# Twenty places for expert weights in place of eighteen, and new homes for the buffers ahead of the expert loop

## The chip, the cores and the metric

The kernel runs on one core of a Trainium2 chip. Its engines work side by side, each on its own stream of instructions, and wait for one another on semaphores: PE (TensorE, matrix products), DVE (VectorE), ACT (ScalarE), POOL (GpSimd) and SP (SyncE, which here only issues loads and stores). Data lies in DRAM, in SBUF (128 partitions, from which the engines read) and in PSUM, where PE leaves its results. Sixteen DMA engines move data between DRAM and SBUF. The metric is the time of one execution in microseconds (us) on the device; lower is better. A MB of weights is 1,048,576 bytes here; megabytes in the profile are millions of bytes.

## The reference

One streaming step of an encoder layer for 288 tokens (256 of a prompt, 32 of a sample) with 1024 channels, all in 32-bit floats. A conditioning vector for each of the two groups gives shifts, scales and gates. Ahead of the experts stand a normalization, an input projection, a pooling mixer, a convolution module, sigmoid gates and an output projection. What takes most of the time is the last part, a mixture of 32 experts, of which each token is given to four:

```python
h2 = RMSNorm(x) * (1 + scale2(c)) + shift2(c)
logits = (h2 @ router_w + router_b); top_vals, top_idx = top_k(logits, 4); top_w = softmax(top_vals)
for e in range(32):
    gt = minimum(t @ exp_w_gate[e] + exp_b_gate[e], 7.0)
    up = clip(t @ exp_w_up[e] + exp_b_up[e], -7.0, 7.0)
    act = gt * sigmoid(1.702 * gt) * (up + 1.0)
    out = out + combine[:, e:e + 1] * (act @ exp_w_down[e] + exp_b_down[e])
y = RMSNorm(x + gate2(c) * out)
```

Each expert has three matrices of 1024 x 1024 floats, 4 MB each, so the weights of all 32 are 384 MB, and each byte is used for the few tokens that chose the expert.

## The kernel before

**The front** is everything up to the router. Its weights come in 46 pieces of up to 1 MB (`FRONT`), in the order in which PE uses them, into a ring of twelve places of 1 MB. SP issues the loads; the load of a piece waits until PE has used what lay in its place, which PE counts in the semaphore `piece_used`. The other buffers of the front lie in one large tile, `arena`, as views at fixed offsets; several views share the same bytes at different times. The tokens `x` and the normalized tokens `h2` are tiles of their own.

**The experts.** Tokens are gathered into groups of at most 64 for one expert; such a group is an item. There are at least 32 items, and one more for each expert that has over 64 tokens. One item (`item`) is three products on PE (gate, up, down), each over four pieces of 1 MB; beside them stand the scatter of the item before, the gather of the next item, and transposes. DVE and ACT do the clamps, the sigmoid and the sums in between. The matrices of an expert come in six pairs of pieces: gate 0 and 1, up 2 and 3, down 4 and 5. Pairs are numbered through all experts (`q`), and pair q goes to place q modulo `PAIRS`: the six pairs of places of the ring, and three pairs of places in the arena, EARLY, LATE and LAST. With nine pairs and six to an expert the assignment repeats after three experts (`TURN`), so the loops of PE and SP are written out for three experts, run ten times, and two experts follow behind. An expert's items are an inner loop whose bounds are read from a table.

**The order of the loads on SP** is one queue. Behind the last pieces of the front come the pairs of expert 0 in the order 5, 0, 1, 2, 3, 4, each when PE has used what lay in its places of the ring; pair 4 in two halves. Between pairs 1 and 2 comes the first pair of expert 1, into EARLY (it waits for the convolution's activations and two more). After pair 4 come the second pair of expert 1 into LATE, when the logits of all tokens are there (`logit_mm`), and the third into LAST, when the last tokens are normalized (`h2_ready`). Then SP waits for the table of the items (`base_ready`) and from there on refills places (`refill`): pair q is loaded when PE has used pair q - 9. The first three of these go in halves (`refill_halves`, `HALVED`).

**Around the change on ACT and DVE.** ACT spreads rows of the modulation from DRAM to all partitions (`spread`: `g1b`, `sh2b`, `a2b`). DVE adds the output projection to `x` (`add_output`), normalizes (`norm2`) first the sample rows (tile 2) and later tile 0, and picks experts (`choose`). ACT takes squares and roots in between. Copies of the sample rows to `xs` stand on ACT right ahead of the loop.

Of the kernel before, what the change touches and what calls it, by code (L numbers as in the profile page):

```python
# [24 lines left out]
P = 128  # L25
# [30 lines left out]
ARENA = 17660  # L56
EARLY_PAIR, LATE_PAIR, LAST_PAIR = ARENA - 4096, 7168, 3072
# [3 lines left out]
PAIRS = 9  # L61
TURN = 3
SPLIT, HALVED, LAST_HALVES = 4, 3, (1, 2, 3, 5)
# [22 lines left out]
def build(nc, x_prompt, x_sample, state_pool, state_conv, c_prompt, c_sample, norm1_g, norm2_g, final_g,  # L86
# [3 lines left out]
    with ExitStack() as ctx:  # L90
# [8 lines left out]
        x = sb("x", [P, TT, D])  # L99
        h2 = sb("h2", [P, TT, D])  # L100
# [10 lines left out]
        c_cols = sb("c_cols", [P, 2 * KD])  # L111
# [5 lines left out]
        csig = sb("csig", [P, 16])  # L117
# [29 lines left out]
        hT = view(0, KD, TOK)  # L147
        gates = view(2304, 2 * KD, TOK)
        hS = view(2304, KD, TOK)
        shT = view(8064, KD, 32)  # L150
        group_of = view(8320, TOK)
        pick = view(8608, 2, 2)
        merged = view(6912, KD, TOK)
        sig_g = view(6912, CT, TOK)
        up_ext = view(9216, CT, PEXT)
        pooled = view(10488, CT, TOK)
        wsum = view(11640, 2, PEXT)
        rows = view(12288, 3, HALF)
        tmp = view(13824, CT, CW)
        act_c = view(9216, CT, TOK)  # L160
        slot_i = view(13824, SLOTS).bitcast(I32)
        part_i = view(13824 + SLOTS, SLOTS).bitcast(I32)
        n2rows = view(15120, HALF)[0:64, :]
        bada = view(15632, HALF)[0:4, :]
        ada_sel = view(16144, 4, 32)[0:4, :, :]
        ada_bias = [view(16912, HALF), rows[:, 0, :]]
        stage = view(16528, P)[0:N_COLS, :]
        c_stage = view(16656, P)[0:2 * KD, :]
        dwc = view(16784, CT, 32)
        h2flat = h2[:, :, :].rearrange("p a b -> p (a b)")  # L170
        uc_ext = h2flat[:, 0:CT * CEXT].rearrange("p (a b) -> p a b", b=CEXT)
        yc = h2flat[:, CT * CEXT:CT * CEXT + CT * CW].rearrange("p (a b) -> p a b", b=CW)


        g1b = view(0, 2, D)
        a2b = view(2304, 2, D)
        sh2b = view(4352, 2, D)
        g2h = biases[:, 1, :].rearrange("p (a n) -> p a n", a=2)
        x2T = view(9216, KD, 2 * P)
        x2T_s = cT  # L180
        rw_g = [view(2048, KD, E), rw]
        junk = view(6400, HALF)
        junk2 = view(11776, HALF)
        ysb = view(11264, 2, HALF)
        xs = view(12672, D // 4)
        part_sum = view(13504, 4)
        xg = view(0, HALF)
        xgT = view(512, HALF)
        ohwT = view(12288, TT * P)
        gmin = view(1024, HALF)  # L190
        gsig = view(1536, HALF)
        acts = view(2048, HALF)
        actT = view(2560, HALF)
        bias_down = ysb[:, 0, :]
        same_row = view(12928, P)
        y_s = h2[:, 2, 0:D // 4]
        oh = view(13312, TT, SLOTS)
        turned = view(13056, 2 * TT, 32)
        count_b = view(2560, P)[0:E, :]
# [9 lines left out]
        ybuf = h2  # L209
        ln_mean, ln_var = view(6912, CW), view(6912 + CW, CW)  # L210

        def slots(q, k):

            if q < RING:
                return ring[:, q:q + k, :].rearrange("p s n -> p (s n)")
            at = (EARLY_PAIR, LATE_PAIR, LAST_PAIR)[(q - RING) // 2] + SLOT * (q % 2)
            return arena[:, at:at + SLOT * k]
# [5 lines left out]
        far_ld = [sem(f"far_ld{i}") for i in range(3)]  # L223
        pair_ld = slot_ld[0:RING:2] + far_ld

        def half_at(p):

            return 2 * p + 1 if 2 * p < RING else 2 * p - RING // 2 + 1
# [71 lines left out]
        h2_zero = sem("h2_zero")  # L300
# [153 lines left out]
        def _(sp):  # L454
# [78 lines left out]
            for i, t in enumerate((0, 2, 1)):  # L533
# [4 lines left out]
                elif t == 0:  # L538
                    sp.dma_start(y_prompt[0, 0:P, :], ybuf[:, 0, :]).then_inc(stored, 16)
                else:  # L540
                    for hh in range(2):
                        sp.wait_ge(y_ready, i + 1 + hh)
                        cs = slice(HALF * hh, HALF * (hh + 1))
                        sp.dma_start(y_prompt[0, P:2 * P, cs], ybuf[:, 1, cs]).then_inc(stored, 16)
# [4 lines left out]
        def _(pool):  # L549
# [82 lines left out]
            pool.wait_ge(pm_mm, KD)  # L632
# [4 lines left out]
        def _(act):  # L637
# [12 lines left out]
            for t in range(2):  # L650
                act.wait_ge(x_ld[t], 16)
                a.activation(view(2304 + D * t, D), x[:, t, :], ACT.Square, accum_out=stat[:, t:t + 1]).then_inc(ssq, 1)
# [6 lines left out]
            a.activation(h2[:, 1, :], x[:, 1, :], ACT.Copy, scale=stat[:, 5:6]).then_inc(xn_ready, 1)  # L659
# [95 lines left out]
            def spread(buf, b, at, done):  # L755
                for gg, r in ((0, P), (1, NS_TOK)):
                    act.dma_start(buf[0:r, gg, :], mod_rows[b][gg:gg + 1, D * at:D * (at + 1)].broadcast_to([r, D])) \
# [30 lines left out]
            a.activation(h2[0:NS_TOK, 2, :], x[0:NS_TOK, 2, :], ACT.Square, accum_out=stat[0:NS_TOK, 2:3]).then_inc(ssq2, 1)  # L788
            act.wait_ge(ssq2, 1)
            root(2, 1)  # L790
            for hh in range(2):
                cs = slice(HALF * hh, HALF * (hh + 1))
                act.wait_ge(x2_ready, 2 + hh)
                a.activation(h2[:, 0, cs], x[:, 0, cs], ACT.Square, accum_out=stat[:, 12 + hh:13 + hh]).then_inc(ssq2, 1)
# [4 lines left out]
            root(0, 2)  # L799
            act.wait_ge(x2_ready, 4)  # L800
# [63 lines left out]
        def _(dve):  # L864
# [16 lines left out]
            squares = view(2304 + 2 * D, D)[0:NS_TOK, :]  # L881
# [13 lines left out]
            for t in (0, 2):  # L895
                r = ROWS[t]
                v.tensor_scalar(h2[0:r, t, :], x[0:r, t, :], stat[0:r, 4 + t:5 + t], None, ALU.mult).then_inc(xn_ready, 1)
# [120 lines left out]
            v.memset(h2[:, 2, :], 0.0).then_inc(h2_zero, 1)  # L1018
# [43 lines left out]
            v.memset(item_col[:, :, :], 0.0)  # L1062
            dve.wait_ge(rows_out[1], 64)
            step(v.memset(oh, 0.0))
            step(v.memset(rt[:, 6, 2, :], 1.0))

            dve.wait_ge(h2_zero, 1)
            wo_reads = [0]

            def add_output(r, t, cuts, after=0):  # L1070
# [3 lines left out]
                parts = [view(12288 + cs.start, cs.stop - cs.start)[0:r, :] for cs, _ in cuts]  # L1074
                for part, (cs, src) in zip(parts, cuts):
                    v.tensor_tensor(part, src, g1b[0:r, t // 2, cs], ALU.mult).then_inc(wo_ev, 1)
# [6 lines left out]
            def norm2(t):  # L1083

                r, gg = ROWS[t], t // 2
                step(v.scalar_tensor_tensor(out=h2[0:r, t, :], in0=x[0:r, t, :], scalar=stat[0:r, 4 + t:5 + t],
                                            in1=a2b[0:r, gg, :], op0=ALU.mult, op1=ALU.mult))
                v.tensor_tensor(h2[0:r, t, :], h2[0:r, t, :], sh2b[0:r, gg, :], ALU.add).then_inc(h2_ready, 1)
# [39 lines left out]
            choose(2, 1)  # L1128
            dve.wait_ge(ssq2, 3)
# [747 lines left out]
```

## Time and profile before

| what | us |
|---|---|
| three runs | 1151.28, 1152.16, 1153.07 |
| median of the runs | 1152.16 |
| the profiled execution, first to last instruction (span) | 1150.3 |
| median less span, taken for what lies around it | 1.9 |
| PE busy | 1122.8 (98%) |
| DVE, ACT, POOL busy | 497.9 (43%), 181.4 (16%), 29.8 (3%) |
| moved by DMA | 456.15 MB, mean 397 GB/s |

The profile is of one execution. Its page shows the span in 40 equal slices of 28.8 us; a chain of waits, followed back from the last instruction, says at each moment what the end was waiting for; groups and timelines give single instructions by line, engine and operation, with the tiles that they write and read (out<-in) and, in brackets, the idle time ahead of them and what ended it. ACTq and SPq are the instructions by which ACT and SP issue DMA; their duration is that of the issue, not of the transfer. In a row with xN the duration runs from the start of the first of the N to the end of the last. Matmuls of PE are pipelined; each 32-bit product counts as two matmuls and two weight loads (PEld).

### The profile page before, as it was taken

The numbers are of one execution on the slowest core, as the hardware profiler recorded it, in microseconds if no ns is written. First come the engines' busy times: TensorE is split into PE (matmuls) and PEld (weight loads), VectorE is DVE, ScalarE is ACT, GpSimd is POOL, SyncE is SP. The second block draws the span as 40 slices with busy tenths as digits, with TensorE's granted clock in tenths as the row PEclk, the third lists the DMA queues.
The fourth block names the chain that finished last, engine by engine and source line by source line (L and its number), as shares of the span: only waits on it lengthen the run. The fifth ranks groups of instructions, "written<-read, shape, count | busy, mean of one in ns | idle before, by whom it ended". The sixth has DMA issues, their size and how long they took to land.

```text
span 1150.3 us, 16135 instructions
## 1 busy us (share of the span) xinstructions
PE 1122.8 (98%) x5962; PEld 457.5 (40%) x5963; DVE 497.9 (43%) x1134; ACT 181.4 (16%) x343; POOL 29.8 (3%) x78
## 2 busy tenths in 40 slices
PE   8999999999999999999999999999999999999996
PEld 6676675633333333333333333333333333333332
DVE  3498425653344433444333433343334433333334
ACT  4101301311111111111111111111111111111112
POOL 4002300000000000000000000000000000000000
PEclk9999999999999999999999999999999999999999
DMA  9988688699999999999999999999999999999995
GB/s 342 374 288 297 245 305 303 229 419 417 427 428 428 428 428 428 428 428 428 428 428 428 428 428 428 428 428 428 428 428 428 428 428 428 428 428 429 426 422 228
DMA packets 59022, 456.15 MB, mean 397 GB/s; under 512 B 7237, under 2 KB 26497, under 8 KB 31349
## 3 DMA queue, kind: packets, MB, share of 16 engines
q1 hardware_dynamic: 54880, 452.35, 94.9%
q10 hardware_dynamic: 4117, 3.47, 1.2%
q8 instruction: 16, 0.26, 0.1%
q14 instruction: 9, 0.07, 0.0%
HBM read 454.40 MB, written 1.40 MB: 396 GB/s over the span
## 4 chain that ended last, share of the span: by engine, by line
PE 77%; DMA 21%; DVE 1%; issue 0%; SPq 0%; ACT 0%; DVEq 0%
PE bank L1731 46%; DMA arena<-in_exp_w_up 10%; DMA arena<-in_exp_w_gate 10%; PE bank L1509 6%; PE bank L1456 4%; PE bank L1758 4%; PE bank L1675 4%; PE bank L1596 2%; PE bank L1813 1%; PE bank L1579 1%; PE bank L1683 1%; PE bank L1430 1%; PE bank L1749 1%; PE bank L1687 1%; PE bank L1378 1%; PE bank L1689 0%
## 5 line engine op out<-in xcount | busy, mean ns | idle before, releaser
L1731 PE MATMUL bank<-ring,arena 128*64 128x512 f32 x2112 | 469.9, 595 | 10.2 <-DMA ring<-in_exp_w_gate 9.7
L1731 PEld LDWEIGHTS bank<-ring,arena 128*64 128x64 f32 x2112 | 146.3, 137 | 310.0 <-issue 283.7
L1731 PE MATMUL bank<-arena 128*64 128x512 f32 x1056 | 235.9, 595 | 4.2 <-DMA arena<-in_exp_w_gate 4.0
L1731 PEld LDWEIGHTS bank<-arena 128*64 128x64 f32 x1056 | 73.6, 137 | 153.8 <-issue 138.5
L821 ACT ACTIVATE arena<-arena 32x256 f32<-32x256 f32 x136 | 56.0, 412 | 421.1 <-DVE arena L1200 419.9
L1291 DVE TENSOR_SCALAR arena<-bank 128x512 f32<-128x512 f32 x33 | 22.8, 691 | 166.6 <-PE bank L1731 166.6
L1284 DVE TENSOR_SCALAR arena<-bank 128x512 f32<-128x512 f32 x33 | 22.8, 691 | 166.5 <-PE bank L1731 166.5
L1306 DVE TENSOR_TENSOR arena<-bank,biases 128x512 f32<-128x512 f32 x66 | 42.5, 686 | 109.9 <-PE bank L1731 109.9
L1269 DVE TENSOR_TENSOR x<-x,bank 128x512 f32<-128x512 f32 x132 | 84.5, 681 | 12.6 <-PE bank L1758 12.6
L834 ACT ACTIVATE arena<-arena 128x512 f32<-128x512 f32 x33 | 20.8, 629 | 353.8 <-DVE arena L1284 353.8
L1758 PE MATMUL bank<-arena 64*128 64x512 f32 x264 | 65.6, 615 | 0.0
L1509 PE MATMUL bank<-arena,ring 128*128 128x288 f32 x256 | 64.4, 409 | 0.0
L1675 PE MATMUL bank<-h,arena 128*64 128x512 f32 x268 | 63.3, 592 | 0.0
L969 DVE SCALAR_TENSOR_TENSOR h<-h,arena 128x318 f32<-128x318 f32 x120 | 55.5, 541 | 0.0
L1509 PEld LDWEIGHTS bank<-arena,ring 128*128 128x128 f32 x256 | 48.1, 190 | 17.1 <-issue 4.2
L1456 PE MATMUL bank<-arena,ring 128*128 128x288 f32 x192 | 47.7, 408 | 0.5 <-DVE arena L922 0.5
L834 ACT ACT_TABLE_LOAD x33 | 42.3, 1283 | 0.6
L1456 PEld LDWEIGHTS bank<-arena,ring 128*128 128x128 f32 x192 | 36.2, 190 | 12.0 <-issue 1.7
L1687 PE MATMUL bank<-biases,mine 32*64 32x288 f32 x264 | 40.0, 414 | 0.0
L1758 PEld LDWEIGHTS bank<-arena 64*128 64x128 f32 x264 | 22.7, 186 | 42.3 <-issue 42.3
L1205 DVE COPY arena<-arena 32x256 f32<-32x256 f32 x136 | 38.4, 282 | 2.5
L1683 PE MATMUL bank<-biases,mine 32*64 32x512 f32 x136 | 37.4, 613 | 0.0
(312 smaller groups left out, 739.8 us busy)
## 6 DMA issues: line engine op xcount, KB each, us to landing
ring<-in_exp_w_gate SPq DMA_DIRECT2D x42, 2048.0 KB, 27.8
ring<-in_exp_w_up SPq DMA_DIRECT2D x41, 2048.0 KB, 28.2
ring<-in_exp_w_down SPq DMA_DIRECT2D x40, 2048.0 KB, 29.1
arena<-in_exp_w_gate SPq DMA_DIRECT2D x21, 2048.0 KB, 25.7
arena<-in_exp_w_up SPq DMA_DIRECT2D x20, 2048.0 KB, 27.3
arena<-in_exp_w_down SPq DMA_DIRECT2D x20, 2048.0 KB, 30.0
ring<-in_w_ada SPq DMA_DIRECT2D x24, 1024.0 KB, 10.7
ring<-in_gate_w SPq DMA_DIRECT2D x8, 1024.0 KB, 8.6
```

Source lines behind the costliest of these rows:

```text
L821: ins = a.activation(*square_moves(1, s, u), ACT.Copy)
L834: a.activation(gsig, gmin, ACT.Sigmoid, scale=ALPHA).then_inc(gsig_ready, 1)
L969: ins = v.scalar_tensor_tensor(out=yc[:, c, :], in0=uc_ext[:, c, k:k + CW], scalar=tap, in1=yc[:, c, :], op0=ALU.mult, op1=ALU.add)
L1269: ins = v.tensor_tensor(x[:, t, cs], x[:, t, cs], scatter_bank(t, hh), ALU.add)
L1306: v.tensor_tensor(ysb[:, gg, :], bank[5][:, :], g2h[:, gg, :], ALU.mult).then_inc(y_ev, 1)
L1456: ins = mm(bank[n % 4][:, 0:TOK], w[:, k, P * (n % 2):P * (n % 2 + 1)], (hS if n < UNSHIFTED else hT)[:, k, :], start=(k == 0), stop=(n >= ...
L1509: ins = mm(bank[n % 4][:, 0:TOK], w[:, k, P * (n % 2):P * (n % 2 + 1)], hT[:, k, :], start=(k == 0), stop=(k == KD - 1))
L1675: ins = mm(bank[0][64 * hh:64 * hh + 64, :], oh[:, t, :], half_rows(h2[:, t, :], hh), start=start, stop=stop, skip_group_check=True)
L1683: mm(bank[3][out, :], mine[B_GATE, :], bias_rows[B_GATE, cs], start=True, stop=False, skip_group_check=True)
L1687: found = mm(bank[6 + i][out, 0:TOK], mine[LOOKUP, :], routedT[:, i, :], start=True, stop=True, skip_group_check=True)
L1731: ins = mm(out[64 * hh:64 * hh + 64, :], lhs(k), w[:, D * (k % 2) + HALF * hh:D * (k % 2) + HALF * (hh + 1)], start=(done is y_mm and k == ...
L1758: ins = mm(scatter_bank(t, hh), ohwT[64 * hh:64 * hh + 64, P * t:P * (t + 1)], ysb[64 * hh:64 * hh + 64, 0, :], start=True, stop=True, ski ...
```

## The change

Nothing that is computed changes. The arena grows from 17660 to 23840 columns and takes in `x` and `h2`, which were tiles of their own; its views are laid out anew, so that four pairs of places lie in it: EARLY as before, SAMPLE where tile 2 of `x` and the sample's modulation rows lie, MERGED where the merged branches lie, and NORM, whose first half holds the convolution's activations and whose second half holds modulation rows of the prompt. That is ten pairs of places. The assignment of pairs now repeats after five experts, and the loops of PE and SP are written out for five, run six times, with two experts behind. The constants and the views (the other views are moved likewise):

```diff
-ARENA = 17660
-EARLY_PAIR, LATE_PAIR, LAST_PAIR = ARENA - 4096, 7168, 3072
+MERGED_PAIR = WEIGHTED_AT + 288
+NORM_PAIR = MERGED_PAIR + 4096
+EARLY_PAIR = NORM_PAIR + 4096
+SAMPLE_PAIR = 2 * D
+ARENA = EARLY_PAIR + 4096
-PAIRS = 9
-TURN = 3
-SPLIT, HALVED, LAST_HALVES = 4, 3, (1, 2, 3, 5)
+PAIRS = 10
+TURN = 5
+SPLIT, HALVED, LAST_HALVES = 4, 2, (1, 2, 3, 5)
+NORM_SPLIT = 9
...
-        x = sb("x", [P, TT, D])
-        h2 = sb("h2", [P, TT, D])
+        x = view(TOKENS_AT, TT, D)
+        h2 = [view(NORMED_AT + D * t, D) for t in range(2)] + [biases[0:NS_TOK, 0, :]]
+        sh2b = [view(NORM_PAIR + SLOT + D, D), view(SAMPLE_PAIR + D, D)]
+        a2b = [view(NORM_PAIR + SLOT, D), view(SAMPLE_PAIR + 2 * D, D)]
+        g1b = [h2[1], view(SAMPLE_PAIR + 3 * D, D)]
```

The loads on SP (`order` is the order 5, 0, 1, 2, 3, 4 of the pairs of expert 0):

```diff
+            def load_half(e, q, half):
+                i, p = q % PER_EXPERT, q % PAIRS
+                w = (wg_v, wu_v, wd_v)[i // 2]
+                sp.dma_start(slots(2 * p + half, 1), w[e][:, i % 2, SLOT * half:SLOT * (half + 1)]).then_inc(pair_ld[p], 16)
...
+                if i == order[4]:
+                    sp.wait_ge(cm_mm, KD)
+                    load_half(1, NORM_SPLIT, 0)
+                    sp.wait_ge(h2_ready, 1)
+                    sp.wait_ge(xs_ready, 1)
+                    load(1, PER_EXPERT + 1)
                 if i == SPLIT:
                     for half in range(2):
-                        sp.wait_ge(piece_used, front_use(i) - 1 + half)
+                        if half:
+                            sp.wait_ge(wo_mm, 6)
+                        else:
+                            sp.wait_ge(piece_used, front_use(i) - 1)
...
-            sp.wait_ge(logit_mm, TT)
-            load(1, PER_EXPERT + 1)
+            sp.wait_ge(ssq2, 6)
+            load(1, PER_EXPERT + 2)
             sp.wait_ge(h2_ready, TT + 1)
-            load(1, PER_EXPERT + 2)
+            load_half(1, NORM_SPLIT, 1)
             sp.wait_ge(base_ready, 1)
```

On the other engines: ACT's copies of the sample rows move up, behind the root of tile 0, and write where the router's weights lay; DVE clears its one-hot tile `oh` behind the choice for the sample and no longer ahead of the output projection, and drops a memset of `h2`; POOL's memset of `bias_down` waits for the merged branches in place of the pooling product; ACT waits for `rows_out` one spread earlier.

```diff
             act.wait_ge(merged_ready, KD)
+            act.wait_ge(rows_out[1], 64)
             spread(sh2b, 0, 1, spread_ld[1])
-            act.wait_ge(rows_out[1], 64)
...
             root(0, 2)
+            act.wait_ge(logit_mm, 1)
+            for q in range(4):
+                ins = a.activation(quadrant(xs, q), quarter(x[0:NS_TOK, 2, :], q), ACT.Copy)
+            ins.then_inc(xs_ready, 1)
             act.wait_ge(x2_ready, 4)
...
             move_squares()
-            act.wait_ge(h2_ready, TT + 1)
-            for q in range(4):
-                ins = a.activation(quadrant(xs, q), quarter(x[0:NS_TOK, 2, :], q), ACT.Copy)
-            ins.then_inc(xs_ready, 1)
...
             choose(2, 1)
+            step(v.memset(oh, 0.0))
```

How this stands on SP, from the last pieces of the front to the table of the items. Before (a place in `ring` or `arena`, the matrix, its shape, and the semaphores that end the wait):

```order
L469 DMA ring<-in_exp_w_down 128x4096 [waits piece_used]
L469 DMA ring<-in_exp_w_gate 128x4096 [waits piece_used] x2
L469 DMA arena<-in_exp_w_gate 128x4096 [waits rows_out2,cst_mm,act_c_ready]
L469 DMA ring<-in_exp_w_up 128x4096 [waits piece_used] x2
L486 DMA ring<-in_exp_w_down 128x2048 [waits piece_used] x2
L469 DMA arena<-in_exp_w_gate 128x4096 [waits logit_mm]
L469 DMA arena<-in_exp_w_up 128x4096 [waits h2_ready]
L510 TENSOR_LOAD base_i [waits base_ready]
```

And on SP now, the same stretch:

```order
L481 DMA ring<-in_exp_w_down 128x4096 [waits piece_used]
L481 DMA ring<-in_exp_w_gate 128x4096 [waits piece_used] x2
L481 DMA arena<-in_exp_w_gate 128x4096 [waits rows_out2,cst_mm,act_c_ready]
L481 DMA ring<-in_exp_w_up 128x4096 [waits piece_used]
L487 DMA arena<-in_exp_w_up 128x2048 [waits cm_mm]
L481 DMA arena<-in_exp_w_gate 128x4096 [waits xs_ready,h2_ready]
L481 DMA ring<-in_exp_w_up 128x4096 [waits piece_used]
L514 DMA ring<-in_exp_w_down 128x2048 [waits piece_used]
L514 DMA ring<-in_exp_w_down 128x2048 [waits wo_mm]
L481 DMA arena<-in_exp_w_up 128x4096 [waits ssq2]
L487 DMA arena<-in_exp_w_up 128x2048 [waits h2_ready]
L538 TENSOR_LOAD base_i [waits base_ready]
```

A half for NORM and a whole pair for SAMPLE have moved between the two up pairs of expert 0, and behind the down halves there are a pair for MERGED and the other half for NORM, where there were two pairs.

On ACT, from the squares of the sample rows to the squares of tile 1, before:

```order
L788 ACTIVATE h,stat<-x 32x1024 [waits x2_ready]
L784 ACTIVATE stat<-stat 32x1 [waits ssq2]
L794 ACTIVATE h,stat<-x 128x512 [waits x2_ready]
L797 ACTIVATE arena<-bank 128x4x128 [waits x2_turned]
L794 ACTIVATE h,stat<-x 128x512 [waits x2_ready]
L784 ACTIVATE stat<-stat 128x1 [waits mean2]
L801 ACTIVATE arena,stat<-x 128x512 [waits x2_ready]
```

And on ACT now (`x` and `h2` are part of `arena`, the normalized sample rows of `biases`, `xs` of `rw`):

```order
L816 ACTIVATE biases,stat<-arena 32x1024 [waits x2_ready]
L812 ACTIVATE stat<-stat 32x1 [waits ssq2]
L822 ACTIVATE arena,stat<-arena 128x512 [waits x2_ready]
L825 ACTIVATE arena<-bank 128x4x128 [waits x2_turned]
L822 ACTIVATE arena,stat<-arena 128x512 [waits x2_ready]
L812 ACTIVATE stat<-stat 128x1 [waits mean2]
L830 ACTIVATE rw<-arena 32x256 [waits logit_mm]
L830 ACTIVATE rw<-arena 32x256 x3
L833 ACTIVATE arena,stat<-arena 128x512 [waits x2_ready]
```

Four copies have moved in between the root of tile 0 and the squares of tile 1.

## Rows read from the trace of the kernel before

**Rows 1.** The page: span, GB/s in 40 slices, a group of the loop.

```profile
span 1150.3 us, 16135 instructions
...
GB/s 342 374 288 297 245 305 303 229 419 417 427 428 428 428 428 428 428 428 428 428 428 428 428 428 428 428 428 428 428 428 428 428 428 428 428 428 429 426 422 228
...
L1291 DVE TENSOR_SCALAR arena<-bank 128x512 f32<-128x512 f32 x33 | 22.8, 691 | 166.6 <-PE bank L1731 166.6
```

**Rows 2.** Stretches: PE, PEld, DVE, ACT, POOL busy (count); PE clock, DMA share, GB/s.

```profile
197.30:209.00 11.70, 11.70 (x51) 6.16 (x50) 5.50 (x14) 1.61 (x4) 0.00 (x0) 1.00 0.02 7
...
219.00:220.50 1.50, 1.50 (x13) 1.33 (x12) 1.36 (x4) 0.87 (x3) 0.00 (x0) 1.00 0.03 11
220.50:231.00 10.50, 10.15 (x70) 5.71 (x72) 8.80 (x39) 6.74 (x14) 0.00 (x0) 1.00 0.99 370
231.00:246.50 15.50, 15.50 (x78) 5.11 (x76) 9.65 (x32) 0.63 (x1) 0.00 (x0) 1.00 1.00 419
246.50:270.00 23.50, 23.50 (x130) 8.12 (x128) 9.76 (x22) 3.97 (x7) 0.00 (x0) 1.00 1.00 407
...
300.00:1100.00 800.00, 786.27 (x4180) 266.81 (x4178) 310.60 (x668) 115.19 (x203) 0.00 (x0) 1.00 1.01 428
```

**Rows 3.** Chain that ended last, 300 to 1130 us: start, us, what.

```profile
542.80 38.62 DMA arena<-in_exp_w_gate
...
1070.74 39.47 DMA arena<-in_exp_w_gate
1110.35 7.09 PE bank L1731 x32
```

**Rows 4.** Stretches of one item each, from the loop's start (columns as above).

```profile
228.88:255.82 26.94, 26.94 (x144) 9.39 (x146) 14.98 (x47) 5.94 (x10) 0.00 (x0) 1.00 1.00 416
...
309.69:336.62 26.93, 26.93 (x146) 9.26 (x144) 10.71 (x23) 3.97 (x7) 0.00 (x0) 1.00 1.01 428
```

**Rows 5.** SP's issues, 120 to 320 us: start, us, engine, line, op, tiles.

```profile
181.96 27.10 SPq L469 DMA_DIRECT2D ring<-in_exp_w_up  x2
214.37 5.74 SPq L486 DMA_DIRECT2D ring<-in_exp_w_down  x2
221.31 0.33 SPq L469 DMA_DIRECT2D arena<-in_exp_w_gate  x1
224.70 0.33 SPq L469 DMA_DIRECT2D arena<-in_exp_w_up  x1
230.86 2.05 SPq L513 DMA_DIRECT2D ring<-in_exp_w_up  x2
234.29 8.12 SPq L513 DMA_DIRECT2D ring<-in_exp_w_down  x4
246.53 6.59 SPq L469 DMA_DIRECT2D ring<-in_exp_w_gate  x2
```

**Rows 6.** Timeline of ACT and DVE: start, us, operation, idle ahead and its end.

```profile
182.40 2.33 ACTq L757 DMA_DIRECT2D arena<-mod_rows  x4
...
197.21 1.27 DVE L1086 SCALAR_TENSOR_TENSOR h<-x,stat,arena 32x1024 f32<-32x1024 f32 x1 [3.32 <-DMA arena<-mod_rows]
...
202.51 0.29 ACT L784 ACTIVATE stat<-stat 128x1 f32<-128x1 f32 x1 [0.59 <-DVE stat L1130]
...
208.31 0.69 DVE L1132 COPY arena<-bank 128x512 f32<-128x512 f32 x1 [5.83 <-PE bank L1606]
...
213.01 0.63 ACT L801 ACTIVATE arena<-x 128x512 f32<-128x512 f32 x1 [10.21 <-DVE x L1080]
...
227.88 1.69 ACT L828 ACTIVATE arena<-x 32x256 f32<-32x256 f32 x4
```

**Rows 7.** Instruction queues (PE's is q8) in 228.9-309.7, 309.7-1085, 1085-1150.3 us.

```profile
q8 instruction: 4, 0.07, 0.3%
...
q14 instruction: 1, 0.01, 0.0%
...
q8 instruction: 3, 0.05, 0.3%
```

More of the change, by code:

```diff
@@ L144, in view @@
             return a
[L147 to L177, printed above, removed]
+        def front(start, *shape):
+            return view(FRONT_AT + start, *shape)
+        x = view(TOKENS_AT, TT, D)
+        xn = view(OLD_ROWS_AT, TT, D)
+        uc_ext = view(OLD_ROWS_AT, CT, CEXT)
+        yc = view(OLD_ROWS_AT + CT * CEXT, CT, CW)
+        hT = view(OLD_ROWS_AT + 2688, KD, TOK)
+        gates = front(2304, 2 * KD, TOK)
@@ new lines, in build @@
+        hS = front(2304, KD, TOK)
+        shT = front(8064, KD, 32)
+        group_of = front(8320, TOK)
+        pick = front(8608, 2, 2)
+        merged = front(6912, KD, TOK)
+        sig_g = front(6912, CT, TOK)
+        up_ext = front(9216, CT, PEXT)
+        pooled = front(10488, CT, TOK)
+        wsum = front(11640, 2, PEXT)
+        rows = front(12288, 3, HALF)
+        tmp = front(13824, CT, CW)
+        act_c = front(9216, CT, TOK)
+        slot_i = front(13824, SLOTS).bitcast(I32)
+        part_i = front(13824 + SLOTS, SLOTS).bitcast(I32)
@@ new lines, in build @@
+        n2rows = front(15120, HALF)[0:64, :]
+        bada = front(15632, HALF)[0:4, :]
+        ada_sel = front(16144, 4, 32)[0:4, :, :]
+        ada_bias = [front(16912, HALF), rows[:, 0, :]]
+        stage = front(16528, P)[0:N_COLS, :]
+        c_stage = front(16656, P)[0:2 * KD, :]
+        dwc = front(16784, CT, 32)
+        c_cols = front(17424, 2 * KD)
+        csig = front(17440, 2 * KD)
+        h2 = [view(NORMED_AT + D * t, D) for t in range(2)] + [biases[0:NS_TOK, 0, :]]
+        sh2b = [view(NORM_PAIR + SLOT + D, D), view(SAMPLE_PAIR + D, D)]
@@ new lines, in build @@
+        junk2 = view(MERGED_PAIR + D, HALF)
+        parts_of = view(MERGED_PAIR, D)
+        ysb = view(Y_AT, 2, HALF)
+        xs = rw[:, :, :].rearrange("p k e -> p (k e)")
+        part_sum = cT[:, KD - 1, 28:32]
+        xg = view(WORK_AT, HALF)
+        gmin = xg
+        xgT = view(WORK_AT + HALF, HALF)
+        gsig = view(WORK_AT + 2 * HALF, HALF)
+        acts = view(WORK_AT + 3 * HALF, HALF)
+        actT = acts
+        ohwT = view(WEIGHTED_AT, TOK)
+        bias_down = ysb[:, 0, :]
@@ L208, in build @@
         routedT = biases[LOOKUP, 0, 0:2 * TOK].rearrange("p (a n) -> p a n", a=2)
-        ybuf = h2
-        ln_mean, ln_var = view(6912, CW), view(6912 + CW, CW)
+        ln_mean, ln_var = front(6912, CW), front(6912 + CW, CW)
         def slots(q, k):
@@ L222, in build @@
         slot_ld = [sem(f"slot_ld{s}") for s in range(RING)]
-        far_ld = [sem(f"far_ld{i}") for i in range(3)]
+        far_ld = [sem(f"far_ld{i}") for i in range(4)]
         pair_ld = slot_ld[0:RING:2] + far_ld
         def half_at(p):
-            return 2 * p + 1 if 2 * p < RING else 2 * p - RING // 2 + 1
+            return 2 * p + 1 if 2 * p < RING else 2 * p - RING // 2 - 1
         piece_used = sem("piece_used")
@@ L651, in _ @@
                 act.wait_ge(x_ld[t], 16)
-                a.activation(view(2304 + D * t, D), x[:, t, :], ACT.Square, accum_out=stat[:, t:t + 1]).then_inc(ssq, 1)
+                a.activation(front(2304 + D * t, D), x[:, t, :], ACT.Square, accum_out=stat[:, t:t + 1]).then_inc(ssq, 1)
             act.wait_ge(c_cols_ready, 1)
@@ L880, in _ @@
             v.tensor_copy(c_cols[:, :], bank[5][:, 0:2 * KD]).then_inc(c_cols_ready, 1)
-            squares = view(2304 + 2 * D, D)[0:NS_TOK, :]
+            squares = front(2304 + 2 * D, D)[0:NS_TOK, :]
             dve.wait_ge(x_ld[2], 16)
@@ L1073, in add_output @@
                     dve.wait_ge(x2_ready, after)
-                parts = [view(12288 + cs.start, cs.stop - cs.start)[0:r, :] for cs, _ in cuts]
+                parts = [parts_of[0:r, cs] for cs, _ in cuts]
                 for part, (cs, src) in zip(parts, cuts):
-                    v.tensor_tensor(part, src, g1b[0:r, t // 2, cs], ALU.mult).then_inc(wo_ev, 1)
+                    v.tensor_tensor(part, src, g1b[t // 2][0:r, cs], ALU.mult).then_inc(wo_ev, 1)
                 wo_reads[0] += len(cuts)
@@ L1346, in _ @@
             halves = [slice(HALF * hh, HALF * (hh + 1)) for hh in range(2)]
-            finish(1, 3, [(ybuf[:, 1, cs], x[:, 1, cs], fgb[:, cs]) for cs in halves])
+            finish(1, 3, [(h2[1][:, cs], x[:, 1, cs], fgb[:, cs]) for cs in halves])
         @block.tensor
@@ L1688, in gather_strips @@
                                        skip_group_check=True)
-                    ins = mm(bank[0][out, :], oh[0:NS_TOK, 2, :], half_rows(h2[0:NS_TOK, 2, :], hh), start=start, stop=stop, skip_group_check=True)
+                    ins = mm(bank[0][out, :], oh[0:NS_TOK, 2, :], half_rows(h2[2], hh), start=start, stop=stop, skip_group_check=True)
                 if lookup:
```

78 lines of the change are left out of this document (33 added, 45 removed).

## The prediction

> **What bounds the kernel now.** I read the page's row of GB/s by slice first [rows 1]. The reader is to see two regimes in it: a front of eight slices (some 230 us) at 229 to 374 GB/s with dips, and then 27 slices that all say 427 to 429. In the stretch from 300 to 1100 us the 16 DMA engines are busy the whole time at 428 GB/s, while PE is busy 786.27 of 800 us [rows 2]. Two engines that both look full: one of them must be following the other. The chain of waits says which [rows 3]: around 543 us the time is handed to loads of expert weights, and so again at the end: the last item starts at 1110.35 us, when a gate pair that was issued at 1070.74 has landed 39.47 us later. Between these PE runs at its own pace: an item takes 26.94 us and the next 26.93 [rows 4]. An expert is 12 pieces of 1 MB (1.0486 million bytes), 12.58 MB, and at 428 GB/s takes 29.4 us to load. So PE is the faster of the two by 2.5 us an expert and lives off a lead that the loads have when the loop begins.
>
> How far is PE from being the bound? There are 33 items, since an operation that is done once an item counts x33 [rows 1]. The loop starts at 228.88 us (the first matmul of the stretch that begins there); 32 items of 26.935 us would have the last one start at 1090.8, and it starts at 1110.35 [rows 3]. PE has 19.5 us to spare. What ends the kernel is the time at which the DMA engines have moved the weights, and that is: total bytes at 428 GB/s, plus every microsecond in which the engines stand idle. After 231 us they hardly do (419, 407, 428 GB/s [rows 2]). So the change is worth what it takes off the idle time ahead of the loop, and all of it reaches the end as long as it is under 19.5 us.
>
> **Where the engines stand idle before.** From 197.3 to 209.0 us their share is 0.02 and from 219.0 to 220.5 it is 0.03 [rows 2], which is 11.5 + 1.5 = 13.0 us. The queue of SP shows why [rows 5]. The first of the two up pairs goes out at 181.96 and the second at 208.73 (181.96 + 27.10 - 0.33), because its place in the ring holds a piece of the output projection that PE still reads. All free places are full and nothing may be loaded. The next are a half at 214.37, its other half at 219.78, then pairs at 221.31 and 224.70, and at 230.86 the first refill, which waits for the loop itself.
>
> **The change, part by part.** (1) A tenth pair of places, 2.10 MB. At 428 GB/s this is 4.90 us. It can be filled ahead of 231 us only if the engines have room there, and they have 13.0 us.
>
> (2) The order of the loads. The half for the normalization pair goes right behind the load at 181.96 and lengthens the busy stretch that ended at 197.3 by 1.05 MB / 428 = 2.45 us, to 199.8. The sample pair waits for the normalized sample rows and for their copy on ACT. The copies are the four that take 1.69 us at 227.88 [rows 6], moved up behind the square root that ended at 202.80. I reckon their time from the rows spread from DRAM, for which DVE waited until 197.21 [rows 6]. With 2.45 us more in front of them they land at up to 199.7, everything on DVE until the square root moves by that much plus some 0.3 us for the cleared one-hot tile that is now in between, and the copies end at about 207.4 (204.8 if the rows land as before). From there 2.10 (sample) + 2.10 (up) + 1.05 + 1.05 (halves) + 2.10 (merged) + 1.05 MB = 9.45 MB are queued one behind the other, released at 207.4, 208.73, 214.37, then at some 219.8 and 221.3 (the second half and the merged pair wait for the last output product and the last square now; I leave them at the times of the half and the pair that went there) and 224.7. That is 22.1 us of transfer, which ends near 230.2. At 230.86 the first refill follows. So the idle 11.5 us shrink to about 8, the 1.5 us at 219 go, and all twenty places are full at the time when before 2 MB of eighteen were still on their way.
>
> (3) What else is moved is beside other work. DVE has 5.83 us of idle time before its copy at 208.31 [rows 6], and gives up 2.45 + 0.3; if this cover were gone, each further microsecond would move the loop's start by one. ACT idles 10.21 us before 213.01 [rows 6] and takes in copies of 1.69. The two memsets that go from DVE and the later memset on POOL are off every chain here; I cost them at nothing. SP's queue is in order: the up pair stands behind the sample pair's two waits, which are met at 207.4 by the sum above, and the up pair was free at 208.73 only. PE reads it in the second product of the first item, over 20 us after that (228.88), so some ten microseconds more would be hidden. The later second halves of refills (two pairs in halves, no longer three) release 1 MB 1.7 us later, once.
>
> (4) How much of the lead stays. From 230.86 on requests come as fast as PE frees places, and a DMA queue that is ahead runs dry. Before: 11 MB in 1 MB units (11.53 MB) were requested from 219.78 until just ahead of 246.53 [rows 5], and 370 x 10.5 + 419 x 15.5 = 10.38 MB were moved [rows 2], so 1.15 MB were outstanding there. One pair more at 246.53, none until 252.79 (246.53 + 6.59 - 0.33) [rows 5], at 407 GB/s: 0.70 MB left, 1.6 us. This is the thinnest point. With the tenth pair the engines can be ahead of before by at most 2.10 + 0.70 = 2.80 MB there, 6.5 us, and by 2.10 MB, 4.9 us, if they keep the same 0.70 MB in flight. The trace of before has no queue that runs dry in the loop; the nearest row is the restart at 220.5, where 370 in place of 428 GB/s over 10.5 us cost 1.4 us. From below I therefore take 4.9 - 1.4 = 3.5, from above 6.5, and as the value 5.2, near the row of the plain capacity.
>
> Sum: -5.2 us, from the profiled execution's 1150.3 to 1145.1. It stands 1.9 us under the median of the runs (1152.16), which is what lies around the span, so the median becomes 1147.0.
>
> (5) The loop of five experts. What runs does not change, but the code that PE jumps back over grows by 5/3. The nearest rows are of PE's instruction queue [rows 7]: four packets of 16 KB in the first turn of three items, none from 309.7 to 1085 us (one packet of another engine's queue, q14, is all there), three when the last two experts' code begins. So all four stay on the engine through nine further turns, and the item after the first jump back takes the same 26.93 us [rows 4]. With five experts 4 x 5/3 = 6.7 must stay, which no row shows. If they don't, each of the five jumps back waits for a packet. From below such a wait is nothing; a packet's own time is 0.3% x 16 x 80.8 us / 4 = 1.0 us; from above it is the longest wait of a small transfer that I find, 197.21 - 182.40 = 14.8 us for the spread rows [rows 6]. I take nothing, since PE's remaining 19.5 - 5.2 = 14.3 us hide five waits of up to 2.9 us, and a lone packet is nearer to 1.0 than to 14.8.
> The Trainium skill, page "Runtime: NRT & Kernel Launch", section "Instruction fetch mechanics", has the rule for this: PE's instruction memory holds 128 KiB and is refilled in blocks of 16 KiB, and a taken branch to code it no longer holds waits for a fetch. By its figure, eight blocks, the new loop with one block ahead would have an estimated 7.7 of 8 and just fit; the sum would be the same. The same section says that the memory is two lines only, by which the old loop would have fetched at every turn; the trace (no packet in 775 us) is against that.
>
> **Rivals.** First, slower: the five experts' code does not stay. The place is the jump at the end of a turn, the price five waits, and it decides from 2.9 us each. At 5 us each it is 25 - 14.3 = 10.7 us behind the forecast, 1157.7; at the upper bound 1207. For it: 6.7 packets is the most any row here would have to bear. Against: four stayed with no sign of a limit, and a packet is short. That it is not resident I hold for 0.25 or so; that a wait then costs over 2.9 us for half of that, and over 4.4 (from where the kernel ends over 1154.5) for a third.
>
> Second: the half pair in front of the spread rows hurts the chain to the loop. If these land 9 us later in place of 2.45, DVE's cover is exceeded by some 3.5 us, the loop and the refills start that much later, and 5.2 - 3.5 leaves 1150.5. For it: the DMA row shows 16 engines fully busy while these rows wait. Against: 1 MB is 2.45 us of transfer.
>
> Third, it does not do what it says: PE is the bound, and loads that come sooner change nothing, 1152.2. For it: PE is 77% of the chain by length and 98% busy. Against: the 19.5 us above, and the loads at the end of the chain.
>
> **Chances.** Forecast 0.76, with its own range 1145.5 to 1148.7 (a lead of 6.5 to 3.5 us). Instruction fetch that shows 0.13, of which 0.09 ends over 1154.5. The late chain 0.07, PE as the bound 0.04. Within 0.2%, 2.3 us, no measurement of this kernel tells a difference. So faster 0.78 (the forecast and the mild end of the late chain), same 0.12, slower 0.10. The range 1144.5 to 1151.5 takes in the forecast, the late chain and a queue that starts a little better than I reckon.
>
> **What would show it.** Right: the share of the stretch 200 to 208 us near zero, and none idle at 219; a short dip at 230 to 232; all ten pairs landed ahead of 232; a first item that still starts near 228.9 and items of 26.9 us, also after the first jump back (near 363 us now); loads that bind PE later than 543 us, since a lead of 5 us lasts two items more; the last item starting near 1105. Wrong: packets of PE's instruction queue between 370 and 1080 us, or PE idle at every fifth item; a loop start after 230; a dip of many microseconds in the GB/s between 231 and 260.

## The result and the profile after

The changed kernel takes 1184.41 us, the median of four runs (1182.77 to 1189.18), against 1151.78 us (1151.28 to 1153.07) for the kernel before: the ratio is 1.0283, with a 95% interval from 1.0263 to 1.0302. It is 2.8% slower, where the prediction had 1147.0 us and 1151.5 as the end of its range.

The page of the changed kernel answers to [rows 1]. It gives the span, the granted clock and the GB/s in 40 slices of 29.6 us, PE's instruction queue over the whole span (packets, MB, share), the chain by engine, and the costliest group (busy time and mean ns, then idle time ahead of it and what ended it).

```profile
span 1182.8 us, 16078 instructions
...
PEclk9999999999998999989999989999899998999999
...
GB/s 348 376 252 298 251 307 298 340 377 429 426 428 426 426 428 428 426 426 428 426 428 423 290 328 427 427 427 427 428 427 426 429 426 426 427 428 427 428 401 59
...
q8 instruction: 63, 1.03, 0.4%
...
PE 95%; issue 3%; DVE 1%; DVEq 0%; POOL 0%; ACT 0%; POOLq 0%
...
L1757 PE MATMUL bank<-ring,arena 128*64 128x512 f32 x1888 | 424.9, 605 | 39.2 <-issue 39.1
```

Three things are new. The chain holds no load any more: it is PE, and 3% "issue", time in which PE waited for nothing that the profile shows. The expert products have 39.2 us of idle time ahead of them, all of it "issue". And two slices in the middle fall to 290 and 328 GB/s, where the loads ran at 428 before: the next load waits for PE to give up a place there (28.4 us in the longest wait of SP between 640 and 720 us). Once PE has lost enough, it is the bound.

The chain of the changed kernel says where the "issue" lies (start, us, what; an x32 is one of an item's three products):

```profile
231.37 7.09 PE bank L1757 x32
...
366.26 7.93 issue
374.19 9.40 PE bank L1757 x32
...
511.40 7.95 issue
519.35 8.51 PE bank L1757 x32
...
682.59 7.39 issue
689.98 8.53 PE bank L1757 x32
...
826.31 7.85 issue
834.16 9.81 PE bank L1757 x32
...
971.78 7.98 issue
979.76 8.71 PE bank L1757 x32
...
1163.12 7.04 PE bank L1757 x32
```

Five gaps of 7.4 to 8.0 us, 144 to 171 us apart, which is five items, or six where an expert has two: the five jumps from the end of a turn to its start. The stretches of the changed kernel (columns as in [rows 2]) show the front, then the items around the first jump, then the gap in steps of 2 us:

```profile
197.30:209.00 11.70, 11.70 (x46) 5.69 (x45) 5.11 (x13) 3.17 (x8) 0.00 (x0) 1.00 0.42 107
...
339.32:366.26 26.94, 26.94 (x145) 8.98 (x140) 10.72 (x23) 3.98 (x7) 0.00 (x0) 1.00 1.01 427
366.26:403.43 37.17, 29.24 (x144) 11.02 (x146) 10.72 (x23) 3.98 (x7) 0.00 (x0) 0.86 1.01 426
403.43:430.37 26.94, 26.94 (x146) 9.25 (x144) 10.72 (x23) 3.98 (x7) 0.00 (x0) 1.00 1.01 428
...
366.00:368.00 2.00, 0.26 (x2) 0.00 (x0) 1.66 (x5) 0.00 (x0) 0.00 (x0) 1.00 0.96 401
370.00:372.00 2.00, 0.00 (x0) 0.18 (x1) 0.00 (x0) 0.00 (x0) 0.00 (x0) 0.50 1.02 426
374.00:376.00 2.00, 1.81 (x6) 0.78 (x7) 0.00 (x0) 0.00 (x0) 0.00 (x0) 0.50 0.98 418
380.00:382.00 2.00, 2.00 (x12) 0.91 (x10) 0.00 (x0) 0.00 (x0) 0.00 (x0) 1.00 1.00 426
```

The item behind the jump takes 37.17 us, its neighbours 26.94 [rows 4]: 10.23 us more. Of these 7.93 are the gap. The other 2.3 come from TensorE's clock, which was granted in full up to the gap, fell to 0.50 (1.2 of 2.4 GHz) in the idle time, and was back in full at 380 us: the first product behind the gap takes 9.40 us in place of 7.09. Behind the other four gaps it takes 8.51 to 9.81. Across the gap the DMA engines go on at full rate, so it isn't weights that PE waits for.

The timeline of the changed kernel in the gap (start, us, operation, idle ahead and what ended it):

```profile
370.23 0.18 PEld L1757 LDWEIGHTS bank<-ring,arena 128*64 128x64 f32 x1 [4.85 <-issue]
374.19 9.40 PE L1757 MATMUL bank<-ring,arena 128*64 128x512 f32 x32 [7.93 <-issue]
374.19 0.29 PEld L1757 LDWEIGHTS bank<-ring,arena 128*64 128x64 f32 x3 [3.78 <-issue]
```

It is two waits of about 4 us: after the first, PE loads weights once, and then stands again for 3.78 us. The other four gaps are split in the same way. PE's instruction queue in the first turn of five experts (231.3 to 366.3 us), and from the first jump to the second (365 to 510.5):

```profile
q8 instruction: 8, 0.13, 0.4%
...
q8 instruction: 9, 0.15, 0.4%
```

Nine packets of 16 KB are fetched in the second turn as in each later one, 63 in all; the kernel before fetched none in its turns after the first [rows 7]. Three of the nine start close to the jump, at 365.8, 371.7 and 378.3 us.

The account has two sides. 32 items of 26.935 us from 231.37 would put the last item at 1093.3 us. Its down product starts at 1163.12 and its gate product, in the trace, at 1143.03. So PE has lost 49.7 us by then, 9.9 for each jump. Read jump by jump, the five gaps are 39.1 us and the five products behind them 9.5 us over 7.09 each, together 48.6, which leaves 1.1 us for the rest of the loop. PE had 19.5 us to spare, and the loop began 2.5 us later than before (231.37 to 228.88): 49.7 - 19.5 + 2.5 = 32.7 us, where the two spans differ by 32.5 (1182.8 - 1150.3).

### The profile page after: what moved, and what is told of

It is laid out like the page before. It is cut to its first block, busy times and chain, and to the rows that moved or that the text cites. A ratio compares the mean times of both kernels' runs of the same rounds, so it can differ in the third digit from the quotient of the medians.

```text
span 1182.8 us, 16078 instructions
## 1 busy us (share of the span) xinstructions
PE 1131.3 (96%) x5962; PEld 468.8 (40%) x5963; DVE 497.4 (42%) x1133; ACT 181.6 (15%) x343; POOL 30.0 (3%) x78
## 4 chain that ended last, share of the span: by engine, by line
PE 95%; issue 3%; DVE 1%; DVEq 0%; POOL 0%; ACT 0%; POOLq 0%
PE bank L1757 59%; PE bank L1535 5%; PE bank L1784 5%; PE bank L1701 5%; PE bank L1482 4%; PE bank L1622 2%; PE bank L1839 2%; PE bank L1709 2%; PE bank L1775 2%; PE bank L1605 1%; PE bank L1456 1%; PE bank L1383 1%; PE bank L1713 1%; PE bank L1404 1%; PE bank L1715 1%
## 5 line engine op out<-in xcount | busy, mean ns | idle before, releaser
L1757 PE MATMUL bank<-ring,arena 128*64 128x512 f32 x1888 | 424.9, 605 | 39.2 <-issue 39.1
L1757 PE MATMUL bank<-arena 128*64 128x512 f32 x1280 | 281.8, 594 | 0.0
L1757 PEld LDWEIGHTS bank<-ring,arena 128*64 128x64 f32 x1888 | 139.2, 139 | 306.1 <-issue 302.6
L1757 PEld LDWEIGHTS bank<-arena 128*64 128x64 f32 x1280 | 89.5, 137 | 178.8 <-issue 175.7
L1310 DVE TENSOR_SCALAR arena<-bank 128x512 f32<-128x512 f32 x33 | 22.8, 692 | 198.9 <-PE bank L1757 198.9
L1317 DVE TENSOR_SCALAR arena<-bank 128x512 f32<-128x512 f32 x33 | 22.8, 692 | 164.0 <-PE bank L1757 164.0
L1295 DVE TENSOR_TENSOR arena<-arena,bank 128x512 f32<-128x512 f32 x132 | 84.6, 682 | 12.6 <-PE bank L1784 12.6
L1701 PE MATMUL bank<-arena,cT 128*64 128x512 f32 x268 | 63.3, 592 | 0.0
L997 DVE SCALAR_TENSOR_TENSOR arena<-arena 128x318 f32<-128x318 f32 x120 | 55.5, 547 | 0.0
```

Of the source, the lines that this page charges most:

```text
L997: ins = v.scalar_tensor_tensor(out=yc[:, c, :], in0=uc_ext[:, c, k:k + CW], scalar=tap, in1=yc[:, c, :], op0=ALU.mult, op1=ALU.add)
L1295: ins = v.tensor_tensor(x[:, t, cs], x[:, t, cs], scatter_bank(t, hh), ALU.add)
L1701: ins = mm(bank[0][64 * hh:64 * hh + 64, :], oh[:, t, :], half_rows(h2[t], hh), start=start, stop=stop, skip_group_check=True)
L1757: ins = mm(out[64 * hh:64 * hh + 64, :], lhs(k), w[:, D * (k % 2) + HALF * hh:D * (k % 2) + HALF * (hh + 1)], start=(done is y_mm and k == ...
```

## The experiments

The theory: the code of five experts doesn't stay on the engine, and all of the loss is the jumps. The rivals: the new homes or the new order of loads cost the time; or it isn't the amount of code, but where in its packet of 16 KB the loop begins. Each ratio is to the kernel before, timed beside the run on the same chip.

**Code alone, in the old layout.** The kernel before, with its loop written out for six experts in place of three:

```diff
-TURN = 3
+TURN = 6
```

> The kernel before with one number changed: the loops of PE and SP are written out for six experts in place of three (nine pairs, the same places, the same loads). Theory 1 (PE's code of a longer loop does not stay on the engine; each jump back fetches it again and the item behind it takes 10.5 us longer, as in the changed kernel, where 359.24 to 396.65 us is 37.4 in place of 26.9): five turns, four jumps back, 4 x 10.5 = 42 us, less the 19.5 us that PE has to spare, so about 1174 us and over 50 packets in PE's instruction queue in place of 16. Rival (the stall belongs to the new places, the new order of loads or ten pairs): 1152 us, 16 to 20 packets, no item over 30 us behind a jump.

Measured: 1174.23 us (1172.1 to 1179.21), ratio 1.0177 [1.016, 1.0194], +21.1 us. Places, homes and loads are those of before. Its chain:

```profile
397.41 8.35 issue
405.76 8.88 PE bank L1731 x32
...
569.37 7.53 issue
...
767.22 7.78 issue
...
938.32 7.92 issue
```

Four jumps, four gaps of the same size, and 59 packets, ten of them in the second turn. Gaps of 7.5 to 8.4 us and first products that take some 2 us more are 39.3 us, of which 19.5 are hidden by PE's spare time. The length of the loop's code is enough to cause the loss.

**Homes and order alone.** The changed kernel with nine pairs and turns of three (the half of the normalization pair isn't loaded then):

```diff
-PAIRS = 10
-TURN = 5
-SPLIT, HALVED, LAST_HALVES = 4, 2, (1, 2, 3, 5)
+PAIRS = 9
+TURN = 3
+SPLIT, HALVED, LAST_HALVES = 4, 3, (1, 2, 3, 5)
...
-                    sp.wait_ge(cm_mm, KD)
-                    load_half(1, NORM_SPLIT, 0)
...
-            load_half(1, NORM_SPLIT, 1)
```

> The changed kernel with nine pairs and a loop of three experts again: the new homes of all buffers and the new order of the loads stay, but the NORM pair is not used. Theory 1: no stall at the jumps, 16 packets in PE's instruction queue; the loads run earlier in the front but into no more places, so the lead is at most the 0.70 MB that were outstanding at the thinnest point, 0 to 1.6 us: 1150 to 1152 us. Rival (new homes or order cause the stall): stalls stay at each of nine jumps, over 1200 us.

Measured: 1153.08 us, ratio 1.0003 [0.9994, 1.0013]. No gap at a jump. Its stretches, and the start of its last item from its chain:

```profile
197.30:209.00 11.70, 11.70 (x50) 6.06 (x49) 4.51 (x14) 3.16 (x8) 0.00 (x0) 1.00 0.29 91
219.00:220.50 1.50, 1.50 (x16) 1.45 (x14) 1.36 (x4) 0.89 (x3) 0.00 (x0) 1.00 0.72 257
220.50:231.00 10.50, 10.18 (x73) 5.84 (x74) 8.82 (x38) 5.08 (x10) 0.00 (x0) 1.00 0.76 299
```

```profile
1110.04 7.09 PE bank L1754 x32
```

The homes and the order do no harm, and without the tenth pair they gain nothing: the loads start earlier (share 0.29 where it was 0.02), the eighteen places are full sooner, and the engines then idle between 219 and 231 us (0.72 and 0.76). The last item starts at 1110.04, before at 1110.35 [rows 3].

**The same loop, begun elsewhere.** The changed kernel with waits ahead of its PE program that are met at once; two of them make one instruction:

```diff
+            for _ in range(200):
+                pe.wait_ge(const, 2)
```

> The changed kernel with 100 instructions more on PE near its start, waits that are already met, in a place where PE waits anyway. They shift the loop's code by 100 instructions of the 256 that a packet holds. Theory 1a (what must stay is counted in whole packets of 16 KB, and the loop of 6.2 packets touches eight of them where it lies now and seven where it lies then): no stall, about 18 packets in all, 1147 us as first forecast, up to 1150 if PE starts the loop later. Theory 1b (the length of the loop alone decides): the same five stalls, 1184 us.

The second has 512 in place of 200, 256 instructions:

```diff
-            for _ in range(200):
+            for _ in range(512):
```

> The same with 256 instructions more, a whole packet: the loop lies within its packets as in the changed kernel. Theories 1a and 1b: both five stalls and 1184 us. Rival to 1a (the added waits themselves do something, such as giving PE a pause at the start): as with 100.

Measured with 100 more instructions: 1157.24 us (1156.6 to 1162.52), ratio 1.0038 [1.0018, 1.0058]. That is 27 us faster than the changed kernel, with more to do ahead of the loop and not one instruction of the loop changed. The item behind its first jump, its first transposition at the start of the program, and its instruction queue in the first turn (241.9 to 376.7 us):

```profile
376.69:403.62 26.93, 26.93 (x146) 9.27 (x144) 10.71 (x23) 3.98 (x7) 0.00 (x0) 1.00 1.01 427
```

```profile
12.69 0.25 PE L1391 MATMUL bank<-ident,arena 16*128 16x16 f32 x1 [6.75 <-issue]
```

```profile
q8 instruction: 6, 0.10, 0.3%
```

No gap, and six packets in the first turn in place of eight; from 373.7 to 1104.2 us there is none. The waits themselves cost more than I had reckoned: PE stands for 6.75 us at the start, and the loop begins at 241.96 in place of 231.37. That is why it isn't faster than before. At 231.28 us PE is 6.5 us behind the changed kernel; the other 4.1 us come right ahead of the loop, where this execution's granted clock was 0.50 from 231.3 to 245.0 us (ten filler matmuls there take 2.50 us, in the changed kernel 1.38). The profiled execution took 1161.82 us, so the median of 1157.24 may not contain this second part.

Measured with 256 more: 1207.86 us (1205.95 to 1210.35), ratio 1.0469 [1.0452, 1.0487]. The gaps are back (64 packets, five gaps of 7.6 to 8.6 us); one of them, and the start of the loop, in its chain:

```profile
255.19 7.09 PE bank L1759 x32
...
390.08 7.57 issue
```

It is 23.5 us slower than the changed kernel (21.4 by the two ratios), and the loop starts 23.8 us later (255.19 to 231.37): that is the waits' own time, for which PE stands 23.88 us at the start and which my expectation had left out. So the same loop stays or doesn't, by where its code begins. The Trainium skill, page "Runtime: NRT & Kernel Launch", section "Instruction fetch mechanics", gives 256 instructions to a block of 16 KiB. By that rule the 256 shift the loop by a whole block and leave its place within one as it was. The two runs agree: one packet more in all, and gaps at all five jumps in both.

**The loop moved the other way, for less.** PE runs products that fill time ahead of the loop (`fill`); done as one of 512 columns in place of four of 128 they cost 80 instructions less (the page has PE x5922 and PEld x5923 in place of x5962 and x5963):

```diff
-                for _ in range(count):
-                    mm(out[:, 0:P], ident[:, :], ones[:, :], start=True, stop=True)
+                while count:
+                    n = min(count, 4)
+                    mm(out[:, 0:n * P].rearrange("p (a n) -> p a n", n=P), ident[:, :], ones[:, :].unsqueeze(1).broadcast_to([P, n, P]),
+                       start=True, stop=True)
+                    count -= n
```

> The changed kernel with 80 instructions fewer on PE ahead of the loop: the filler products of PE in the front (of an identity with ones, to keep PE at work) are issued 512 columns at a time in place of 128, with the same columns in all. The loop's code then ends 80 instructions earlier, in the seventh packet that it touches. Theory 1a (whole packets of 16 KB count, seven and the one fetched ahead stay, eight do not): no packet in PE's instruction queue between the first turn and the last experts, no item over 30 us, and the loop starts as early as before, unlike with 100 waits more (which cost the front some 9 us); what is left is the lead of the tenth pair, 3.5 to 6.5 us: 1145.5 to 1149. Theory 1b (length alone) is as good as fallen by the run with 100 waits: 1184. Rival 2 (the tenth pair brings nothing even without the stall): 1152.

The same edit in the kernel before, as a control:

> The kernel before with the same filler products of 512 columns, to see what these do by themselves. All theories: within 1 us of before, 1151 to 1153; if they change the front or PE's clock there, that shows here and is to be taken off the other run.

Measured: with the change 1149.24 us (1147.23 to 1150.69, nine runs), ratio 0.9958 [0.9943, 0.9974]; in the kernel before 1152.79, ratio 0.9993 [0.9977, 1.0008]. The edit by itself is worth nothing that shows; with it, the change is faster than the kernel before, by some 0.4%. Stretches of the changed kernel with wide filler products, to be laid beside [rows 2]:

```profile
197.30:209.00 11.70, 11.70 (x47) 5.66 (x46) 5.11 (x13) 3.16 (x8) 0.00 (x0) 1.00 0.31 73
219.00:220.50 1.50, 1.50 (x13) 1.35 (x12) 0.71 (x3) 0.37 (x1) 0.00 (x0) 1.00 0.91 366
220.50:231.00 10.50, 10.20 (x68) 5.66 (x69) 8.87 (x37) 5.61 (x13) 0.00 (x0) 1.00 1.01 425
231.00:246.50 15.50, 15.50 (x80) 5.12 (x76) 9.61 (x34) 0.63 (x1) 0.00 (x0) 1.00 0.94 347
246.50:270.00 23.50, 23.50 (x132) 8.12 (x129) 10.71 (x23) 3.97 (x7) 0.00 (x0) 1.00 0.99 397
...
364.63:391.56 26.93, 26.93 (x146) 9.26 (x144) 10.71 (x23) 3.97 (x7) 0.00 (x0) 1.00 1.01 428
```

Its chain, and its instruction queue in the first turn (229.9 to 364.6 us):

```profile
229.94 7.09 PE bank L1760 x32
...
581.18 41.54 DMA arena<-in_exp_w_up
...
1063.32 44.07 DMA arena<-in_exp_w_gate
1107.53 7.09 PE bank L1760 x32
...
1127.81 7.04 PE bank L1760 x32
```

```profile
q8 instruction: 6, 0.10, 0.3%
```

The item behind the jump takes 26.93 us, six packets come in the first turn and none between 348.4 and 1086.9 us, and the loads are back in the chain. The mechanism is the one that I had forecast; the time is 2.2 us above the forecast's 1147.0, and 0.2 above what I expected of this run.

**Six experts with wide filler products.** If where the loop begins were all, six experts might stay as well; if the number of packets decides, they can't:

```diff
-TURN = 3
+TURN = 6
```

> The kernel before with a loop of six experts and with filler products of 512 columns, so that the loop begins where it begins in the fastest kernel so far (within its packet), but touches eight packets. Theory 1a (the count of packets touched decides): four stalls of some 10 us, about 1174 us in one look. Theory 1c (it is where in its packet the loop begins that decides: the two kernels that lost the stall began in the first half of one, the three with it at 0.7): no stall, 1152 us.

Measured, one run: 1161.41 us, the kernel before 1153.29 beside it. It stalls at each of the four jumps, with 55 packets, nine of them in the second turn: the loop begins about where that of the kernel that stays begins, and yet does not stay, so the number decides. But the price is another; its chain and its timeline at the first jump:

```profile
391.71 4.33 issue
396.04 8.78 PE bank L1734 x32
```

```profile
396.04 2.45 PE L1734 MATMUL bank<-ring,arena 128*64 128x512 f32 x6 [4.33 <-issue]
```

One wait in place of two, and 4.33 + (8.78 - 7.09) = 6.0 us in place of 10.2. The other three gaps are 3.8 to 4.0 us, so the four jumps cost PE 22.8 us, 3.3 over its spare 19.5; the kernel is 8.1 us slower, and the rest is not accounted for. A second packet is fetched at 397.7 here too, while PE already works on the first. My reading is that this loop begins nearer to the front of its packet, so that the next packet arrives before PE needs it. This is argued from the packets' times and from my count of the code, and no run varies the begin alone to show it. The 1174 us that I expected were too high because I took some 10 us for a jump.

## Why the prediction was wrong

**The step that failed** is (5), the loop of five experts: "I take nothing", since a wait of up to 2.9 us at each of five jumps would be hidden. The waits came, and cost 9.9 us each. It was the first rival, to which I had given 0.13 and, at 5 us a jump, 1157.7 us. Two things were wrong in it.

First, whether. I reckoned by length: 4 x 5/3 = 6.7 packets. What the runs go by is whole packets: those that the loop's code touches, and one that is fetched ahead of its end. I count them from the times at which the packets start, and take it that PE enters a packet when the next one is fetched. In the changed kernel a packet starts at 215.1 us, ahead of the loop's begin at 231.37: PE is then in the packet in which the loop begins, and the one behind it is on its way. Seven more start in the first turn, the last at 363.0, some 3 us ahead of the jump (the eighth of the queue's row, at 365.8, is already the jump's own). That makes nine, and nine are fetched anew in each later turn (the second of the two queue rows above). With wide filler products the packet ahead of the loop starts at 218.2 and only six more follow, up to 348.4: eight, and they stay. With the 100 instructions it is eight too, and six experts make nine or ten, which don't stay. So the edge lies between eight and nine, and whether a loop of this length needs eight or nine hangs on where it begins: 100 instructions more or 80 fewer ahead of it make it eight. A turn of nine keeps none of them, and not just one less: 63 packets on the page of the changed kernel, 19 with the 100 instructions ahead.
The figure that the prediction cited from the Trainium skill (page "Runtime: NRT & Kernel Launch", section "Instruction fetch mechanics"), 128 KiB in blocks of 16 KiB, agrees with an edge at eight; the same section calls the memory a FIFO, and a loop of nine in a FIFO of eight would find each block gone when it comes back to it. My 7.7 "of 8" rounded at neither end of the loop.

Second, how much. I bounded a wait from 1.0 to 14.8 us and took the lower end as nearer, since "a lone packet is nearer to 1.0". It was two waits of 4 us one behind the other, and then a slower clock: a product at half speed after the gap is a term that the sum lacked altogether. A bound that holds the answer doesn't help if the value is taken at the end that is hidden.

**The other steps** can be read from the run with wide filler products, where the code stays.

(1) The tenth pair is worth 4.90 us at most by the forecast. From 197.3 to 231 us the stretches of that run hold the 2.1 MB and more: it has moved 71.9 MB by 231 us, the kernel before 69.1 (sums over stretches from the start).

(2) The order of the loads: an idle time of "about 8" in place of 11.5 us came out as (1 - 0.31) x 11.7 = 8.1, and the idle 1.5 us at 219 are gone (share 0.91). By the step's own terms the copies end at 207.2 and the last transfer near 229.6, where it has 207.4 and 230.2; nothing hangs on this. Nine pairs in the same order gained nothing, so the order by itself is worth nothing here.

(3) What is moved is hidden: the loop starts at 229.94 in this run and at 229.1 with nine pairs, against 228.88. The changed kernel's profile has 231.37: its filler products at the start took nearly twice as long (24 of them in 5.49 us, 2.94 before), and PE is 2.5 us late from there on. That this was the lower clock is not shown, since the profile has no lower granted clock in this stretch. The late chain, the second rival, did not come.

(4) The lead that stays was 5.2 us with bounds of 3.5 and 6.5. The dip behind 231 us is deeper and longer than I said: 347 GB/s for 15.5 us, where [rows 2] have 419, which the prediction had among its signs of being wrong. By 270 us the run is 86.6 - 85.1 = 1.5 MB ahead, 3.4 us, just under my lower end. The ratio gives -4.8 us, with an interval from -6.6 to -3.0; the medians differ by 3.8, and by 3.6 from the control. So the mechanism was right and the value is not told apart from the forecast; the medians and the profile speak for the lower end. The loads bind PE again in the chain from 581.18 us, before from 542.80 [rows 3], one to two items later; the last item starts at 1107.53, for which I had "near 1105".

The third rival, that PE is the bound, was right only of the kernel that stalls: 49.7 us of jumps used up its 19.5 us.

## What to carry to other kernels

Before a loop is written out further, count PE's code of a turn in whole packets of 16 KB, with both ends and one packet ahead, and look at the instruction queue of the kernel at hand: none in later turns means that it stays, and a turn over the edge fetches all of them again. A loop near the edge can be brought back by taking instructions away ahead of it, as 80 fewer did here, and that is to be tried before a change is given up. A wait of 4 to 8 us on PE cost its own length here and then 1.4 to 2.7 us more in the product behind it.

## What the runs showed of the hardware

- A jump back to code that had gone cost 9.9 us on the mean of five: two waits of some 4 us, and 1.4 to 2.7 us more for the product behind them, which began at the granted clock of 0.50. Where only one wait showed, it was 6.0 us at the first jump.
- A loop of nine packets of 16 KB, counted as above, fetched nine in each turn; loops of eight fetched none after the first turn.
- A hundred instructions ahead of a loop made the kernel 27 us faster, and 256 made it 23.5 us slower.
- Waits that are already met are not free on PE: 256 instructions of two waits each moved the loop by 23.8 us, about 0.09 us for an instruction.
